# A mixture-of-experts sweep over 79 token blocks: block list in three parts, a third set of expert weights, and a new test for the second output copy

## What is computed

```python
g_idx = jnp.argmax(g_logits, axis=-1)                      # one of 4 groups
top_vals, top_idx = lax.top_k(e_in_group, TOP_K)           # 2 of its 4 experts
...
a = jnp.einsum('td,edf->tef', hf, w_gate[gi])              # 1024 -> 512
b = jnp.einsum('td,edf->tef', hf, w_up[gi])
hid = jax.nn.silu(a) * b * combine[:, gi, :, None]
out = out + jnp.einsum('tef,efd->td', hid, w_down[gi])     # 512 -> 1024
...
return x + gate2[:, None, :] * y_moe
```

## The kernel before

| core | blocks of experts 0 to 15 | groups | sum |
|---|---|---|---|
| 0 | 4 4 5 5 5 4 5 5 5 6 5 4 4 4 4 4 | 18 19 20 16 | 73 |
| 1 | 5 4 4 4 5 5 4 5 4 5 5 5 4 4 4 4 | 17 19 19 16 | 71 |
| 2 | 4 4 5 4 6 5 5 4 4 4 5 5 4 4 4 4 | 17 20 18 16 | 71 |
| 3 | 5 4 4 4 5 5 5 5 5 4 4 5 4 4 4 4 | 17 20 18 16 | 71 |
| 4 | 5 5 4 5 6 5 6 5 4 4 4 4 5 4 5 4 | 19 22 16 18 | 75 |
| 5 | 5 4 4 4 5 4 5 4 5 4 5 4 5 5 4 4 | 17 18 18 18 | 71 |
| 6 | 4 4 4 4 7 6 6 5 5 5 5 5 3 4 4 4 | 16 24 20 15 | 75 |
| 7 | 4 4 4 5 5 4 6 6 5 4 4 4 4 4 4 5 | 17 21 17 17 | 72 |

## Time and profile before

### The profile page before, as it was taken

One profiled execution on the slowest core, in us unless ns is written; L12 is line 12 of the kernel. 1 busy time (PEld: TensorE's weight loads), 2 busy tenths in 40 slices (PEclk: granted clock), 3 DMA queues, 4 the chain that ended last, 5 costly groups with the idle time before them and its releaser, 6 DMA issues. The chain is left out here.

```text
span 2326.9 us, 36343 instructions; the slowest of 8 cores (2291.8 to 2326.9 us)
## 1 busy us (share of the span) xinstructions
PE 1863.3 (80%) x11023; PEld 951.3 (41%) x11023; DVE 1044.1 (45%) x2271; ACT 875.0 (38%) x1364; POOL 485.4 (21%) x484
## 2 busy tenths in 40 slices
PE   0387899588879978968997887997839888888996
PEld 0233444255335445424444533543524343434443
DVE  1436543255755335655434575545363233333333
ACT  0324741054465335347415346532313222222322
POOL 1101000132100014101003310011413233333432
PEclk9999999688899988989998899999759888988999
DMA  7567546973626574437556362657247788878777
GB/s 113 141 136 127 98 82 130 175 251 109 128 73 109 127 246 153 65 91 136 110 136 244 101 137 64 119 127 195 86 143 177 185 205 212 212 185 183 166 130 146
DMA packets 113762, 334.62 MB, mean 144 GB/s; under 512 B 26628, under 2 KB 56716, under 8 KB 103332
## 3 DMA queue, kind: packets, MB, share of 16 engines
q0 software_dynamic: 67888, 196.29, 44.9%
q1 hardware_dynamic: 45684, 136.01, 17.1%
HBM read 543.67 MB, written 170.67 MB: 307 GB/s over the span
## 5 line engine op out<-in xcount | busy, mean ns | idle before, releaser
L167 PE MATMUL PS<-hT,slot 128*128 128x512 bf16 x2304 | 570.6, 394 | 53.2 <-DVE B L167 21.7
L167 PE MATMUL PS<-slot,B 128*128 128x512 bf16 x1776 | 447.8, 398 | 81.7 <-DMA slot<-w_bf 76.6
L167 PEld LDWEIGHTS PS<-hT,slot 128*128 128x128 bf16 x2304 | 224.9, 101 | 340.9 <-issue 106.7
L167 PEld LDWEIGHTS PS<-slot,B 128*128 128x128 bf16 x1776 | 169.7, 102 | 279.4 <-issue 131.2
L167 ACT ACTIVATE bfh<-PS 128x512 bf16<-128x512 f32 (+2 forms) x431 | 236.0, 590 | 99.4 <-PE PS L167 97.0
L167 PE MATMUL PS<-BB,slot 128*128 128x512 bf16 x1024 | 247.9, 386 | 0.0
L167 ACT ACTIVATE B<-PS 128x1024 bf16<-128x1024 bf16 x79 | 80.9, 1024 | 342.5 <-PE PS L167 327.4
L167 ACT ACTIVATE FH<-PS,cst 128x512 f32<-128x512 f32 x128 | 88.0, 687 | 311.6 <-PE PS L167 311.6
L167 DVE SCALAR_TENSOR_TENSOR bfh<-PS,small,FH 128x512 bf16<-128x512 f32 x79 | 59.3, 751 | 305.4 <-PE PS L167 305.4
L167 POOL TENSOR_TENSOR small<-small 128x1 f32<-128x1 f32 x96 | 78.7, 819 | 525.5 <-DVE small L167 524.7
L167 PE MATMUL PS<-slot,hT 128*128 128x512 bf16 (+1 forms) x768 | 153.7, 352 | 26.4 <-DVE kT L167 14.2
(11 more groups left out here) (168 smaller groups left out, 2324.7 us busy)
## 6 DMA issues: line engine op xcount, KB each, us to landing
slot<-w_bf SPq DMA_DIRECT2D x395, 512.0 KB
w_bf<-w_ch POOLq DMA_DIRECT2D x96, 512.0 KB
B4h<-w_bf SPq DMA_DIRECT2D x79, 512.0 KB
FH<-x SPq DMA_DIRECT2D x32, 512.0 KB
BB<-x SPq DMA_DIRECT2D x32, 512.0 KB
out<-BB SPq DMA_DIRECT2D x32, 512.0 KB
out<-f32a SPq DMA_DIRECT2D x1, 16384.0 KB
out<-out POOLq DMA_DIRECT2D x1, 16384.0 KB
```

The lines of the kernel that those rows point to most:

```text
L167: ins = getattr(eng, name)(*a, **k)
```

## The change

The block list is cut in three lanes instead of two: LANE = 27, and the lanes start at blocks 0, 27 and 53; position p takes block LST[p % 3] + p // 3. A third set of weight buffers is laid over four tiles that the sweep doesn't use otherwise (`etab`, `vaug`, `R2`, `kT`); sets go by p % 3. `w_load` is called one position further ahead: after `d_mm(p)`, parts 4 and 5 of p+3 and parts 0 to 3 of p+4. Before the loop all six parts of positions 1 and 2 and four of position 3 are issued. The scatter chains stay two, by p % 2. The test for the second output copy now compares the largest group, counted in blocks with tokens only, with LANE - 1 = 26, and the row indices of odd positions get the offset of the second copy if it is used; rows without a token go to one of two spare areas by the parity of p.

```diff
-        LANE = (NB + 1) // 2
+        LANE = (NB + 2) // 3
+        LST = (0, LANE, 2 * LANE - 1)
 
         def bid(p):
-            return p // 2 if p % 2 == 0 else LANE + p // 2
+            return LST[p % 3] + p // 3
...
+        kTf = kT[:].rearrange("p a t -> p (a t)")
+        wts.append([etab[:, 0:2048], etab[:, 2048:4096], vaug[:].rearrange("p a b c -> p (a b c)")[:, 0:2048],
+                    R2[:].rearrange("p g t -> p (g t)").bitcast(BF16), kTf[:, 0:2048], kTf[:, 2048:4096]])
+        wts_r.append([K.alias(f"wt2{i}", o) for i, o in enumerate(([r_const], [r_const], r_vb, [r_const], r_kTc + r_xsT, r_kTc + r_xsT))])
...
-        for b0, b1, c0 in ((0, LANE, 32), (LANE, NB, 33)):
-            wop(lambda e: e.tensor_scalar(out=vb[:, b0:b1], in0=bank(pi, NB)[:, b0:b1], scalar1=0.0, scalar2=col[:, c0:c0 + 1],
-                                          op0=ALU.is_equal, op1=ALU.mult), reads=pir)
+        wop(lambda e: e.tensor_scalar(out=vb, in0=bank(pi, NB), scalar1=0.0, scalar2=col[:, 32:33], op0=ALU.is_equal, op1=ALU.mult), reads=pir)
...
-        wop(lambda e: e.memset(fr[:, LANE:LANE + 1], 0.0))
+        for l_ in LST[1:]:
+            wop(lambda e: e.memset(fr[:, l_:l_ + 1], 0.0))
...
-        wop(lambda e: e.tensor_scalar(out=hv[:, 3:4], in0=c4[:, 3:4], scalar1=-1.0, scalar2=float(NB), op0=ALU.mult, op1=ALU.add))
+        wop(lambda e: e.tensor_tensor(out=hv[:, 6:7], in0=cumb[:, 15:16], in1=na[:, 15:16], op=ALU.add))
+        wop(lambda e: e.tensor_tensor(out=hv[:, 3:4], in0=hv[:, 6:7], in1=c4[:, 3:4], op=ALU.subtract))
         wop(lambda e: e.tensor_reduce(out=hv[:, 4:5], in_=hv[:, 0:4], axis=AX.X, op=ALU.max))
-        wop(lambda e: e.tensor_scalar(out=hv[:, 5:6], in0=hv[:, 4:5], scalar1=float(LANE - 3), scalar2=float(OFF), op0=ALU.is_ge, op1=ALU.mult))
+        wop(lambda e: e.tensor_scalar(out=hv[:, 5:6], in0=hv[:, 4:5], scalar1=float(LANE - 1), scalar2=float(OFF), op0=ALU.is_ge, op1=ALU.mult))
...
-        K.op("dve", lambda e: e.tensor_copy(out=idxs[:, 0:LANE], in_=va[:, 0:LANE]), reads=W, writes=[r_ixs])
-        K.op("dve", lambda e: e.tensor_scalar(out=idxs[:, LANE:NB], in0=va[:, LANE:NB], scalar1=hv[:, 5:6], scalar2=None, op0=ALU.add),
-             reads=W, writes=[r_ixs])
+        wop(lambda e: e.tensor_scalar(out=vb, in0=va, scalar1=float(T), scalar2=128.0, op0=ALU.is_ge, op1=ALU.mult))
+        K.op("dve", lambda e: e.tensor_copy(out=idxs[:, 0:NB], in_=va), reads=W, writes=[r_ixs])
+        for l_, l0 in enumerate(LST):
+            c_ = slice(l0 + (l_ + 1) % 2, (LST + (NB,))[l_ + 1], 2)
+            K.op("dve", lambda e: e.scalar_tensor_tensor(out=idxs[:, c_], in0=va[:, c_], scalar=hv[:, 5:6], in1=vb[:, c_], op0=ALU.add, op1=ALU.add),
+                 reads=W, writes=[r_ixs])
...
-            if 0 in cs or p == 1:
+            if 0 in cs:
...
+                K.dma_call("sp", lambda e, c_=c_: e.dma_start(out=wts[p % 3][c_].bitcast(U8), in_=wchunk(c_, bass.ds(
...
-        w_load(1, (0, 1, 2, 3))
-        w_load(1, (4, 5))
+        for p in (1, 2):
+            w_load(p, (0, 1, 2, 3))
+            w_load(p, (4, 5))
...
-        w_load(2, (0, 1, 2, 3))
+        w_load(3, (0, 1, 2, 3))
...
-            if p + 2 < NB:
-                w_load(p + 2, (4, 5))
             if p + 3 < NB:
-                w_load(p + 3, (0, 1, 2, 3))
+                w_load(p + 3, (4, 5))
+            if p + 4 < NB:
+                w_load(p + 4, (0, 1, 2, 3))
```

More of the change, by code:

```diff
@@ L1406, in w_load @@
             for c_ in cs:
-                K.dma_call("sp", lambda e, c_=c_: e.dma_start(out=wts[p % 2][c_].bitcast(U8), in_=wchunk(c_, bass.ds(
+                K.dma_call("sp", lambda e, c_=c_: e.dma_start(out=wts[p % 3][c_].bitcast(U8), in_=wchunk(c_, bass.ds(
                     bass.RuntimeValue.of_register_unchecked(regs[p % 4], min_val=0, max_val=15 * CHB), CHB)),
                                                               bounds_check="skip_entire_dma"),
-                           reads=[r_wbf, r_tab], writes=[wts_r[p % 2][c_]])
+                           reads=[r_wbf, r_tab], writes=[wts_r[p % 3][c_]])
         def x_t(p):
@@ L1434, in gu_half @@
                 K.op("pe", lambda e, kc=kc, c_=c_: e.matmul(
-                    bank(pb), xT[:, kc, :], wts[p % 2][c_][:, (kc % 4) * 512:(kc % 4 + 1) * 512], start=(kc == 0), stop=(kc == 7)),
-                     reads=[xT_r, wts_r[p % 2][c_]], writes=bank_r[pb:pb + 1], inc=(kc % 4 == 3))
+                    bank(pb), xT[:, kc, :], wts[p % 3][c_][:, (kc % 4) * 512:(kc % 4 + 1) * 512], start=(kc == 0), stop=(kc == 7)),
+                     reads=[xT_r, wts_r[p % 3][c_]], writes=bank_r[pb:pb + 1], inc=(kc % 4 == 3))
         def g_mm(p):
@@ L1468, in d_mm @@
                         bank(4 + dh), ht[:, fl * 128:(fl + 1) * 128],
-                        wts[p % 2][c_][:, (fl % 2) * 1024 + dh * 512:(fl % 2) * 1024 + (dh + 1) * 512], start=(fl == 0), stop=(fl == 3)),
-                         reads=[ht_r, wts_r[p % 2][c_]], writes=bank_r[4 + dh:5 + dh], inc=(dh == 1 and fl % 2 == 1) or fl == 3)
+                        wts[p % 3][c_][:, (fl % 2) * 1024 + dh * 512:(fl % 2) * 1024 + (dh + 1) * 512], start=(fl == 0), stop=(fl == 3)),
+                         reads=[ht_r, wts_r[p % 3][c_]], writes=bank_r[4 + dh:5 + dh], inc=(dh == 1 and fl % 2 == 1) or fl == 3)
             b = bid(p)
```

## The result

| | before | after |
|---|---|---|
| median (lowest, highest) | 2332.95 us (2326.46 to 2507.89, 5 runs) | 2303.6 us (2291.7 to 2431.29, 5 runs) |
| ratio to before | 1 | 0.9857, 95% interval 0.9815 to 0.9898 |
| mean of the 8 spans, profiled | 2314.0 us | 2270.8 us |
| largest of the 8 spans | 2326.9 us, core 3 | 2302.0 us, core 2 |

A repeat of the unedited changed kernel (e8_after) gave 2311.69 us, ratio 0.9875 [0.9841, 0.991]. The forecast was 2296 us and "faster"; the sign and the order of size came true.

A forecast was written before the change was run, and what follows sets the result against it. PE bounds the sweep, with late weight loads adding 104 to 126 us on cores 3 to 5. Core 4's load cost falls from 125.9 to 93.5, span 2293.8; with 1.5 around it and 1.6 to the median, 2296 us, range 2256 to 2321.

The forecast's parts named there:

- Free pass 5.85 us, PE bound, the slow clock only behind a wait: Sweep passes without load stalls: PE busy all 5.85 us at granted clock 1.00; clock slows after PE idled.
- rival 4: Fuller PE on all cores lowers the clock, free passes grow; gain gone at granted clock 0.93; chance 0.03.
- Single load 7.4 to 0.5 us: A weight load with no near neighbour: two passes of lead leave 0.5 us of 7.4, bounds 0 and 2.
- Pair 14.5: Two loads at neighbouring positions: 10.5 us of PE wait plus 4 of slow clock, 14.5, bounds 12 and 19.
- Two apart 7: Two loads two positions apart: 7 us with some slow clock, bounds 3 and 10.
- Rival 2: DMA becomes the bound, gathers and scatters fall behind, pairs cost 17, triples 25 us; time 2308 to 2323; chance 0.12.
- Triple 22: Three loads side by side: 22 us together, bounds 16 and 25.
- Start +11.5 on every core: Pass 1 of the sweep waits for its tenth weight part: 9.4 us plus 2 of slow clock, new.
- Cores 4 and 5 last at 2294, core 3 at 2265.5, others under 2280: Spans from summed load costs: core 4 2293.8 us, core 5 2292.4, core 3 2265.5, the others below 2280.
- Rival 1: Neighbouring loads are hidden too, parts arriving at nearly 1.54 us each; kernel between 2228 and 2262 us; chance 0.11.
- Rival 3: A core uses the second output copy, zeroing and adding 16 MB, 85 us for 16.8 MB; 2380 to 2420; chance 0.03.
- Rival 5: It changes nothing: loads go out no earlier, or the start eats the gain; 2323 to 2337 us; chance 0.05.

The follow-up runs named there:

- e8_after: The changed kernel once more, unedited, as a repeat: 2311.69 us, ratio 0.9875 to the kernel before.
- e1b_held: Changed kernel, SP made to wait for PE's down product before issuing weights, giving the two-set kernel's lead: 2334.62 us, ratio 0.9978 to the kernel before.
- e5_sem32: Changed kernel with 32 instead of 16 semaphores for SP's transfers: 2310.83 us, ratio 0.9845 to the kernel before.
- e3_noscatter: Changed kernel issuing only the last of its 79 scatters, all products still made: 2235.75 us (another run 2277.03).

## Why the prediction was right, and where its terms were off

- *Free pass 5.85 us, PE bound, the slow clock only behind a wait:* as forecast; rival 4 fell (free passes stay at 5.85 us, as the first row of the pair shows at a granted clock of 1.00).
- *Single load 7.4 to 0.5 us:* right in mechanism, shown by e1b_held; its size is 2.2 (3.6 in a repeat), above the bound of 2. The sign "single loads leave passes of about 6 us" holds for about half of them; 9 of the 49 leave passes of 11.9 to 14.6 us, and in the one shown DMA is full.
- *Pair 14.5:* 16.7 (17.7, 17.7 and 16.9 in the repeats and e5_sem32). The mis-sized term is "29.7 us for ten parts", with 1.7 of a possible 4.6 added: it is 38.5 at the pair 31 and 32, as q0 takes half of DMA in that time. There PE waits 14.1 us (10.5 forecast), and the slow clock costs 6.4 (4 forecast). The bound of 19 held for the mean.
- *Two apart 7:* 12.7, above the bound of 10, for the same reason. Rival 2 had given 12 for it and 17 for a pair. *Triple 22:* 16.0 to 20.4, under the forecast. Why a third load costs so little more than the second isn't settled.
- *Start +11.5 on every core:* wrong. Pass 1 takes 7.7 to 8.7 us, 2.4 over a free one. Its tenth part was costed at the pair's 29.7 us; on core 2 ten parts are issued from 1731.20 and used at 1752.02, 20.8 us:

```profile
1731.20 5.91 SPq L1415 DMA_DIRECT2D slot<-w_bf  x5
...
1752.02 1.02 PE L167 MATMUL PS<-R,B 128*128 128x512 bf16 x4 [0.33 <-DMA R<-w_bf]
```

On core 3 it is 20.8 us too (1715.84 to 1736.59), the first scatter starts at 1733.2, and q1 has 84% of DMA's time (1718 to 1737 us). In e3_noscatter, without scatters, pass 1 is as long (8.1 us on average, against 8.3).

- *Cores 4 and 5 last at 2294, core 3 at 2265.5, others under 2280:* half right. Core 5 ended last in two runs, at 2290.2 and 2291.4 (2292.4 forecast), core 2 in two. Core 4 took 2271.9 to 2282.9 us. From first scatter to last, over free passes, the forecast had 93.5, 77.5 and 51.5 us on cores 4, 5 and 3; measured are 66.0, 71.4 and 73.6 in the profiled execution. On core 4 it is the triples and the start that were too dear; on core 3 the groups were too cheap (40 forecast, 73.6 measured).
- *Core 2* has no sum in the prediction. By its prices (four pairs, seven single loads, the start) it is 73 us instead of 111.9, a span of 2270; measured is 2302.0. Of these 32 us about 13 are the price of the loads (86.3 for 73), and some 19 are the sweep's start: its first scatter stands at 1749.1 and stood at 1729.6. The prediction took the start from the old trace, core by core, which does not hold: see below.
- *PE's waits for weights on core 3, 30 to 40 us:* 51.3.
- *Rival 1 (pairs hidden)* fell, and e3_noscatter shows what it would have needed. *Rival 2 (DMA the new bound)* is right for the groups and wrong for the rest: half of the single loads are hidden, and scatters wait for PE. *Rival 3* did not happen; its price of 85 us for the copy is 86.4, and its zeros add a wait of 35.8. *Rival 5* fell with e1b_held.

The forecast of 2296 lies 8 us under the measured time, and in part that is luck: the start was too high by 9, a triple by 6, a pair too low by 2, two apart by 6, and the sweep's start on the last core, which the sum didn't have, is worth more than any of them.

## What to carry to other kernels

A deeper prefetch removes what is late because it was issued late; what is late because queues are full stays, and shows in rows where the DMA share is 1.0 at few GB/s. Ask then which transfer holds the engines for few bytes: here the adding scatter, whose rows cost two and a half times a plain one's (3.34 against 1.36 us a block), so leaving padding rows out pays. With the slowest of 8 cores as the metric, forecast a spread and not one core.

## What the runs showed of the hardware

The sweep starts at another time on each core in each run, although the program ahead is the same, and in a pattern: of the cores 0 and 1, 2 and 3, 4 and 5, 6 and 7, one is 13.6 to 20.2 us behind the other, and which one changes (55 of the 56 such pairs in the 14 profiled executions; once it was 5.6 us, in e5_sem32). PE's first transposes of the sweep on cores 2 and 3 of the changed kernel:

```profile
1730.33 1.01 PE L167 MATMUL PS<-ident_b,hT 128*128 128x128 bf16 x8 [10.05 <-DMA hT<-h2d,BB]
```

```profile
1714.04 1.01 PE L167 MATMUL PS<-ident_b,hT 128*128 128x128 bf16 x8 [8.86 <-DMA hT<-h2d,BB]
```

In the kernel before it is 1711.5 and 1725.8, the other way round. Part of it arises in the first 150 us. The same stretch on core 2 and on core 3:

```profile
100.00:150.00 50.00, 23.24 (x84) 9.25 (x85) 10.29 (x28) 7.56 (x12) 5.98 (x8) 0.83 0.99 173
```

```profile
100.00:150.00 50.00, 27.07 (x101) 10.95 (x102) 10.48 (x27) 9.00 (x13) 6.04 (x8) 1.00 1.02 189
```

Core 3 moves 189 GB/s and core 2 173, and over the whole program PE waits 21.7 against 29.5 us for the matrix `w_in`. The Trainium skill (HBM Reference, "Specifications (TRN2)") says that two cores share the bandwidth of one HBM domain; a pair in which one core is served ahead of the other would look like this. That is argued, not shown, and where the other half of the 16 us comes from is open. It bears on the result: core 2 had the groups of the highest price and the late start of its pair in the profiled execution, 16 us that no edit made.
